# The memory attention's keys made inside the long convolutions; final norm, memory and sine layers in one stage

## The reference, cut to what matters

```python
z_pos, window = hyena_pos_features(L)
for i in range(DEPTH):                                   # 2 layers, L = 256, D_MODEL = 1024
    hn = rmsnorm_2(h, ln_mix[i])
    (aq, ak, av, hy, gq, gk, gv, go, glr, gates) = split_cols(hn @ w_in[i], IN_SPLITS)
    ...
    spec = hyena_filter_spectra(z_pos, window, ...)      # two sine layers, then rfft
    y_b = hyena_mixer(hy, hy_conv[i], spec, hy_skip[i]) @ w_br_hyena[i]
    ...
    h = h + memory_cross_attention(rmsnorm_2(h, ln_x[i]), rmsnorm_2(mem, ln_mem[i]), ...)

def hyena_mixer(u, conv_w, spec, skip):
    v, x1, x2 = jnp.split(short_conv(u, conv_w), 3, axis=-1)
    z = x1 * long_conv(v, spec[:, 0], skip[0])
    return x2 * long_conv(z, spec[:, 1], skip[1])

def memory_cross_attention(hn, mn, wq, wk, wv, wo, qn, kn):
    q = rmsnorm_2((hn @ wq).reshape(B, L, X_HEADS, X_HEAD_DIM), qn)
    k = rmsnorm_2((mn @ wk).reshape(B, M, X_HEADS, X_HEAD_DIM), kn)
    v = (mn @ wv).reshape(B, M, X_HEADS, X_HEAD_DIM)
    ...
```

## Time and profile before

| what | us |
|---|---|
| median of 3 runs | 3047.35 (3042.83 to 3047.6) |
| the profiled execution | 3044.04 |
| its span, first to last instruction | 3041.9 |
| convolution of layer 0, first transpose to the next stage's first matmul | 1765.97 to 1805.95 |
| convolution of layer 1 | 2425.16 to 2464.93 |
| memory stage of layer 0, first matmul to the attention's first | 2050.84 to 2139.68 |
| memory stage of layer 1 | 2709.78 to 2798.59 |
| final norm's squares to the spectra stage's first matmul | 1611.24 to 1646.57 |

### The profile page before, as it was taken

One profiled execution on the slowest core, in us unless ns is written; L12 is line 12 of the kernel. 1 busy time (PEld: TensorE's weight loads), 2 busy tenths in 40 slices (PEclk: granted clock), 3 DMA queues, 4 the chain that ended last, 5 costly groups with the idle time before them and its releaser, 6 DMA issues. The chain is left out here.

```text
span 3041.9 us, 43212 instructions
## 1 busy us (share of the span) xinstructions
PE 2835.9 (93%) x17620; PEld 2511.3 (83%) x17625; DVE 2033.1 (67%) x2025; ACT 1505.8 (50%) x1439; POOL 57.6 (2%) x51
## 2 busy tenths in 40 slices
PE   5999998699999999999996889999899899999999
PEld 5799998588888888888883577999899887989898
DVE  6455574588888888888885756566555565665554
ACT  3443453466676766677661225344433326343432
POOL 1000000000000000000000110000000010000000
PEclk7899999699999999999996899999999899999999
DMA  6155540399999999999992333454255433444352
GB/s 185 57 179 180 181 153 15 128 370 333 368 342 347 360 334 373 336 343 365 333 370 71 111 91 110 139 166 139 98 182 187 138 115 108 139 142 136 128 185 103
DMA packets 364963, 619.10 MB, mean 204 GB/s; under 512 B 14632, under 2 KB 201095, under 8 KB 363541
## 3 DMA queue, kind: packets, MB, share of 16 engines
q1 hardware_dynamic: 363644, 611.72, 58.3%
q10 hardware_dynamic: 1178, 5.36, 0.4%
HBM read 611.80 MB, written 5.24 MB: 203 GB/s over the span
## 5 line engine op out<-in xcount | busy, mean ns | idle before, releaser
L351 DVE TENSOR_TENSOR slots_low<-slots,w_hi 128x2048 fp32r<-128x2048 f32 x240 | 549.3, 2292 | 400.0 <-ACT w_hi L340 399.8
L340 ACT ACTIVATE w_hi<-slots 128x2048 fp32r<-128x2048 f32 x240 | 452.1, 1887 | 365.1 <-PE ps L922 192.0
L1248 DVE TENSOR_TENSOR slots_low<-slots,w_hi 128x2048 fp32r<-128x2048 f32 x224 | 504.3, 2287 | 65.2 <-ACT w_hi L1199 65.2
L453 PE MATMUL ps<-x_hi,w_hi 128*128 128x256 f32 x1520 | 446.3, 294 | 53.8 <-DVE x_lo L533 27.6
L453 PE MATMUL ps<-x_lo,w_hi 128*128 128x256 f32 x1520 | 439.9, 289 | 0.0
L453 PE MATMUL ps<-x_hi,slots_low 128*128 128x256 f32 x1520 | 439.4, 289 | 0.0
L1199 ACT ACTIVATE w_hi<-slots 128x2048 fp32r<-128x2048 f32 x224 | 415.9, 1907 | 0.6 <-DMA slots<-in_moe_w_up_dram 0.4
L453 PEld LDWEIGHTS ps<-x_hi,w_hi 128*128 128x128 f32 x1520 | 302.0, 199 | 60.9 <-issue 54.2
L1132 PE MATMUL ps<-slots_low,x_hi 128*128 128x512 f32 x896 | 349.6, 390 | 0.0
L453 PEld LDWEIGHTS ps<-x_lo,w_hi 128*128 128x128 f32 x1520 | 302.2, 199 | 0.3
L453 PEld LDWEIGHTS ps<-x_hi,slots_low 128*128 128x128 f32 x1520 | 301.4, 198 | 0.0
(11 more groups left out here) (535 smaller groups left out, 5353.7 us busy)
## 6 DMA issues: line engine op xcount, KB each, us to landing
slots<-in_moe_w_gate_dram SPq DMA_DIRECT2D x112, 1024.0 KB, 5.1
slots<-in_moe_w_up_dram SPq DMA_DIRECT2D x112, 1024.0 KB, 5.1
slots<-in_moe_w_down_dram SPq DMA_DIRECT2D x112, 1024.0 KB, 4.9
slots<-in_mlp_w_dram SPq DMA_DIRECT2D x64, 1024.0 KB, 5.1
slots<-in_w_in_dram SPq DMA_DIRECT2D x54, 1024.0 KB, 5.3
slots<-in_ffn_w_gate_dram SPq DMA_DIRECT2D x14, 1024.0 KB, 5.0
slots<-in_ffn_w_up_dram SPq DMA_DIRECT2D x14, 1024.0 KB, 5.0
slots<-in_ffn_w_down_dram SPq DMA_DIRECT2D x14, 1024.0 KB, 4.8
```

The costliest lines, as they stand in the source:

```text
L340: act.activation(w_hi[:, s.buffer, 0:s.kt * s.cols], slots[:, s.slot, 0:s.kt * s.cols], ACT.Copy).then_inc(w_hi_done, 1)
L351: dve.tensor_tensor(slots_low[:, s.slot, 0:n], slots[:, s.slot, 0:n], w_hi[:, s.buffer, 0:n].bitcast(F32), ALU.subtract).then_inc(w_lo_don ...
L453: mm = pe.matmul(b[:, t * T:(t + 1) * T], w, xx[:, k, :], **flags)
L1248: dve.tensor_tensor(low[i % NS], raw[i % NS], his[i % R].bitcast(F32), ALU.subtract).then_inc(lo_done, 1)
```

## The change

The four slabs of `x_wk` move in the list from the memory stage to the convolution, one before each layer's first spectrum and three before its second. `hyena` now makes the keys: ACT and DVE split the memory there, PE puts pieces of six matmuls (`fill`) between its other work, DVE multiplies a finished pair with the memory's root, ACT stores it in DRAM. The memory stage loads the stored keys and has 8 slabs. The memory's root is made once, in the new stage `opening`, which also holds the final norm, the memory's transposes and the sine layers. `z` now overwrites the first third of `hc`, the way back uses two PSUM banks and not four, and two constants are loaded with the first block's.

```diff
+            stream.weights(A["x_wk_2"][l][:, 0:256], 256)
+            spectrum(0)
+            stream.weights(A["x_wk_2"][l][:, 256:1024], 256)
+            spectrum(1)
...
-            for name in ("w_out_2", "x_wq_2", "x_wk_2", "x_wv_2", "x_wo_2"):
+            for name in ("w_out_2", "x_wq_2", "x_wv_2", "x_wo_2"):
...
+        def opening(m_tm, w1s, w2s, h2, needs):
...
+                @block.tensor
+                def _(pe):
+                    pe.wait_ge(squared, 1)
+                    for k in range(KD):
+                        mm = pe.matmul(bank(0)[:, 0:T], ones[:, :], sq[:, k, :], start=(k == 0), stop=(k == KD - 1))
+                    mm.then_inc(summed, 1)
+                    pe.wait_ge(*needs)
...
+                    pe.wait_ge(memory_in, 16)
...
+                    pe.wait_ge(mem_inverted, 1 + TT)
+                    for t in range(TT):
+                        mm = pe.matmul(bank(3)[:, t * P:(t + 1) * P], ones[:, :], diagonal[:, t, :], start=True, stop=True)
+                    mm.then_inc(mem_spread, 1)
+                    pe.wait_ge(sined, 1)
...
+                    angle(0)
+                    split_lo(dve, BEFORE_MOE, len(stream.slabs))
+                    dve.wait_ge(rooted, 1)
+                    dve.reciprocal(ms[:, :], ms[:, :]).then_inc(inverted, 1)
...
+                    angle(1)
...
+                    for k in range(KD):
+                        scale(k)
+                    split_lo(dve, BEFORE_MOE + 1, len(stream.slabs))
...
+                    def fill(n):
+                        for _ in range(n):
+                            next(more_keys, None)
...
                         mm.then_inc(turned, 1)
+                        if o:
+                            fill(2)
                         pe.wait_ge(act_out, o + 1)
                         pe.wait_ge(dve_out, o + 1)
...
+                        transform(0)
+                        transform(2)
+                        fill(1)
+                        transform(1)
+                        transform(3)
+                        fill(4)
                         for i, n in enumerate((0, 2, 1, 3)):
                             pe.wait_ge(product, 4 * o + i + 1)
                             for m in range(4):
...
+                            fill((1, 3, 1, 4)[i])
+                    for _ in more_keys:
+                        pass
...
+                    def store(j):
+                        act.wait_ge(key_out, j + 1)
+                        act.dma_start(keys_dram[l][:, 512 * j:512 * (j + 1)], flat(key[:, :, :])).then_inc(keys_stored, 16)
+                    split_hi(act, ahead, len(stream.slabs))
+                    store(0)
+                    act.wait_ge(turned, 2)
+                    act.activation(u[:, 0, :], turn_bank(1, 0), ACT.Copy).then_inc(act_out, 1)
+                    store(1)
+                    split_hi(act, ahead + 1, len(stream.slabs))
+                    store(2)
+                    store(3)
...
+                    def key_to_buffer(j):
+                        dve.wait_ge(w_used, key_slabs[j].used_after)
+                        if j:
+                            dve.wait_ge(keys_stored, 16 * (4 * l + j))
+                        dve.tensor_tensor(key[:, :, :], two(key_bank(j)), wide(rs_m[:, :], 2), ALU.mult).then_inc(key_out, 1)
...
-                        dve.wait_ge(second_, 4 * o + 4)
-                        dve.memset(junk[:, 1:2], 0.0).then_inc(w_used, 1)
+                        if o == 0:
+                            dve.wait_ge(w_used, key_slabs[0].used_after)
+                            dve.wait_ge(second_, 4)
+                            dve.memset(junk[:, 1:2], 0.0).then_inc(w_used, 1)
+                        else:
+                            key_to_buffer(1)
+                        split_lo(dve, ahead + o, len(stream.slabs))
                         for m in range(4):
...
+                    def side_load_k(act, more):
+                        act.wait_ge(keys_stored, 64 * (l + 1))
+                        act.dma_start(flat(k_[:, :, :]), keys_dram[l]).then_inc(more["k_in"], 16)
...
                     linear(srcs, pairs_of(0, [scale_to(q[:, k:k + 2, :], rs) for k in range(0, 8, 2)])
-                           + pairs_of(1, [scale_to(k_[:, k:k + 2, :], rs_m) for k in range(0, 8, 2)])
                            + [(1, [tm(0, 256, scale_rows_to(v[:, :, n * 256:(n + 1) * 256], rcol_m))]) for n in range(4)],
```

More of the change, by code:

```diff
@@ L1426, in _, with hyena @@
                         act.wait_ge(spectra_out, 16 * N)
-        def hyena(hc, skip, dst):
+        def hyena(l, hc, skip, dst):
             dft = K["dft"][:, :].rearrange("p (t s k) -> p t s k", t=TT, s=2)
             idft = K["idft"][:, :].rearrange("p (s k t) -> p s k t", s=2, k=TT)
-            slabs = take(2)
-            with ExitStack() as c, stage("turned", "act_out", "dve_out", "transformed", "first", "second", "product", "back", "skipped", "out") as \
-                    (block, turned, act_out, dve_out, transformed, first_, second_, product, back, skipped, outed):
+            gain = gain_of("ln_mem", 8 * l)
+            slabs = take(6)
+            spectra_slabs, key_slabs = (slabs[1], slabs[5]), (slabs[0], slabs[2], slabs[3], slabs[4])
+            ahead = slabs[5].index + 1
+            with ExitStack() as c, stage("turned", "act_out", "dve_out", "transformed", "first", "second", "product", "back", "skipped", "out",
+                                         "mem_hi", "mem_lo", "key_out") as \
+                    (block, turned, act_out, dve_out, transformed, first_, second_, product, back, skipped, outed, mem_hi, mem_lo, key_out):
@@ L1482, in _ @@
                             if o:
[L1483 removed]
+                                dve.wait_ge(back, 2)
                             dve.tensor_tensor(y[:, k, :], Ak, Fc, ALU.mult).then_inc(first_, 1)
```

306 lines of the change are left out of this document (190 added, 116 removed).

## The result

| what | before | after |
|---|---|---|
| median | 3047.35 us (3042.83 to 3047.66, 5 runs) | 3060.42 us (3055.52 to 3070.82, 5 runs) |
| ratio to before | | 1.0052 (95% interval 1.0038 to 1.0066) |
| profiled execution, span | 3044.04, 3041.9 | 3056.91, 3055.1 |
| mean granted clock of TensorE | 0.956 | 0.950 |

What follows compares the result with a forecast made beforehand. It took PE (TensorE), busy for 93% of the span, as the bound. Per layer +24.1 convolution, +1.0 clock dip and -28.2 memory stage, twice, with -3.3 for the opening, gave -9.5 us: 3037.8 us, range 3026 to 3050.

Steps and rivals of the forecast that it cites:

- Convolution, +24.1 per layer: Convolution with the keys: 64.1 us for 40.0, about the whole 23.0 us of key matmuls and a little more.
- The keys do fill the idle time: Rival: key matmuls fill PE's convolution waits, stage costs some 20 us more, shorter fold wait; 3022 us in all, chance 0.12.
- Store, 2.4 us: Convolution's tail: DVE waits for the third keys' 256 KB store before overwriting the buffer; 2.4 us, bounds 2.1 and 3.9.
- The clock behind the convolution, 1.0 us: Next stage after the convolution: a clock dip behind 3.3 us of PE idle time, put in at 1.0 us per layer.
- The fold's wait, 4.5 us: Memory stage, slab 1: PE idles 4.5 us for GpSimd's fold, taken as 7.5 us long with two splits beside it.
- The attention at full clock, 1.2 us: Memory attention: after only 1.7 us of idle time it starts at full clock, saving 1.2 us per layer.
- Opening, -3.3: Opening as one stage: spectra's first matmul at 1643.3 us and not 1646.57, 3.3 us saved once.
- 2 x (24.1 + 1.0 - 28.2) - 3.3: Whole kernel: two layers of convolution, clock dip and memory stage with its attention, then the opening; -9.5 us.
- such a move by over 1 us: Sign that the prediction is wrong: a stage that nobody touched moves by more than 1 us.
- As long as its bound: Rival: fold, store, dip and token copy waits at their bounds add 4.3 us per layer; gain gone, 3046 us, chance 0.24.
- The slower rival: Clock stays low in the convolution's first turn; at 8 us per layer measurably slower, 3055 us, chance 0.07.
- Theory B: From the experiments: the loss is a cost of keys stored and loaded through DRAM and constants at other addresses.

Runs made afterwards that it cites:

- splits behind z: Changed kernel with the three splits of the convolution's first turn moved behind the second turn's first key product: 3037.17 us, 0.9993 of before.
- two buffers: Changed kernel with each layer's fourth keys written to a tile the convolution no longer needs, so DVE skips the third's store wait: 3038.58 us, 0.9980 of before.
- busy tail: Changed kernel with 24 short matmuls that nothing reads behind each convolution's last key product: 3053.59 us, 1.0028 of before.
- squares first: Changed kernel with ACT's squares of x in the memory stage ahead of the memory's high part: 3048.06 us, 1.0011 of before.

## Why the prediction was wrong, step by step

- **Convolution, +24.1 per layer: right** (+23.8). The splits do hold up z (pairs at 28.4 us into the stage, forecast 28.8; "splits behind z" gets 1.9 and 1.6 us back), and the rest of its order holds within 0.7 us. That the stage came out 0.3 us from the forecast is partly luck: the third keys' product ends 0.7 us earlier than I had it, and the store behind it takes 0.6 us longer. "The keys do fill the idle time" is excluded in this form.
- **Store, 2.4 us: too small.** It took 3.0, issue to landing, and the next key product started 2.75 us after the one ahead of it had ended. It lay between my bounds. The estimate by the Trainium skill's page (DMA: Bandwidth & Descriptors, "Anatomy of one DMA"), 2.6 us, was nearer, and is also too small.
- **The clock behind the convolution, 1.0 us: mis-sized.** The measured price is 2.5 us per layer behind 3.4 us of idle time, 1.5 behind 1.76 ("two buffers"), none behind 0.44 ("busy tail"), and none behind 2.67 in the kernel before. I had priced it by the length of the wait, although my own rows already had a wait of 2.67 us with no fall and one of 2.39 with a fall.
- **The fold's wait, 4.5 us: 5.29.** The fold took 8.48 us; I had taken 7.5 "with two splits". The three rows now known are 4.72 us with no split beside it ("squares first"), 6.51 with one, 8.44 with two: 1.8 and 1.9 us for a split. Of the three splits that I had counted beside the 8.44 of the earlier trace rows, the third began about as the fold ended. The stage took 63.43 and 64.93 us against my 61.9; the wait's 0.8 us are part of that, and the two layers differ in how long the clock stays low behind the fold (3.4 and 6.8 us). That GpSimd contends with VectorE, as the Trainium skill has it (GPSIMD Engine Reference, "Specifications"), the runs bear out.
- **The attention at full clock, 1.2 us: 1.65.** Right in kind.
- **Opening, -3.3: -2.3** in this profile (31.1 us against 33.4). Over all profiles the new opening takes 30.2 to 31.1 us and the old one 32.8 to 33.4, so -1.7 to -3.2.
- **The step that failed** is the sum's silence about stages that the change doesn't touch: "2 x (24.1 + 1.0 - 28.2) - 3.3" has no term for them. Self-attention and the mixers' output product cost 5.8 us more in each layer, 11.6 in all, with the same instructions and waits (within 0.1 us). For self-attention, 4.65 of the 5.8, the cause is shown: TensorE's granted clock is low for 17 us of it and not for 3.4. I had named such a move by over 1 us as a sign that I was wrong, and that sign is what the profile shows first. The mis-sized terms above make a further 2.4 us in layer 0 and 4.0 in layer 1, the MLPs 1.8. With 1.0 less from the opening they turn -9.5 into +11.4; the first block's +4.3 and the spectra's -2.6, both of them in the range of chance, make that the profile's +13.2.
- **The rivals.** "As long as its bound" gave the right kind for the touched stages (4.3 us per layer more; measured 2.4 and 4.0) but not the sign of the whole. The slower rival named the clock, at the wrong place: the convolution's first turn isn't slower than before.

Theory B explains the store's wait and perhaps the MLP's 1.5 us: the other losses vanish in kernels that keep all of the keys' traffic, and one of them shows in a kernel that has none. **Open:** what the chip's clock goes by, so that the same idle stretch is followed by a short fall in one place and a long one in another, alike in both profiles of two programs, while one program's executions come in two kinds and those of the kernel before spread over 11 us (3039.2 to 3050.5 on one chip, mean granted clock 0.959 to 0.954). The experiments show that it does, not why. The Trainium skill (TensorE: Matmul & The Clock Gate, "Part 1: The HAM clock gate") says that the window in which activity is watched runs free of the program. That instants matter agrees with it. That self-attention took 29.66 us in both layers of two executions of the changed kernel (to 0.01 us), and 25.0 us in as many of the kernel before, does not follow from a phase that is free at the start.

## What to carry to other kernels

Where TensorE waits for 2 to 3 us between dense stages, a change anywhere ahead can add or remove time behind the wait: here 1.7 to 4.7 us at self-attention, 1.1 to 2.5 at two other places. Compare the untouched stages of the two traces first, and before judging an edit fill those gaps with a few matmuls of zeros in both versions, or shift the work by a microsecond and see whether the verdict stands. Then read stage by stage: in the kernel before, the same filling saved 2.6 us in self-attention and the total didn't fall, with new losses of some 5 us in layer 1's projection, convolution and attention projection.

Work that moves off a stage can bring a wait and hide another: here the fold, which the memory stage has only with one normed input, and behind it the squares of the keys, which showed once the fold's wait was gone. And in a program written out in order, an engine's idle time ahead of a block is not free for that block; the three splits stood behind a wait of 7 us and still delayed what followed.

## What was unexpected of the hardware

- A stage of the same instructions behind the same wait (2.75 us) took 25.0 or 29.7 us, with the granted clock low for 3.4 or for 17 us, and 23.75 with twelve matmuls of zeros ahead of it and six in it, where the clock was never low.
- Eight short matmuls a layer, 0.86 us on the path, made a kernel 11 us longer; four made no difference.
- A wait of 1.76 us was followed by a fall of the clock, and one of 2.67 us at the same place in another version of the kernel was not.
- A higher clock can lengthen a stage: it moved a DVE split into GpSimd's fold, 8.44 us for 6.51, and PE waited 2.17 us for it (2.10 in the changed kernel).
